# Hybrid encoder layer on one Trainium2 core: the short convolution's projections leave the head loop and become 2x2-block pairs, and GpSimd combines the two attention maps

## The reference

```python
proj = u @ w_in                      # u: normalised x; columns: h, b, c (512 each), q, k, v (512 each), gates (2048)
inner = cc * hc
conv = sum(pad(inner)[:, tap:tap + s] * conv_w[tap] for tap in range(3))
y_conv = (bc * conv) @ w_conv_out
# 4 heads, query blocks of 128 tokens, two maps per head
s1 = q1b @ k1.T * scale + bias;  s2 = q2b @ k2.T * scale + bias
a = softmax(s1) - lam * softmax(s2)
o = rmsnorm(a @ v) * (1 - lam_init)
y_attn = o @ w_attn_out
merged = g[0] * y_conv + g[1] * y_attn          # g = sigmoid(gates + b_gate)
x = x + norm(merged @ w_o)
x = x + norm(relu(norm(x) @ w_ff1) ** 2 @ w_ff2)
```

## Time and profile before

| | before |
|---|---|
| median of 3 runs | 1377.86 us (1377.61 to 1378.33) |
| span of the profiled execution | 1375.7 us |
| TensorE busy | 1366.8 us (99%) |
| VectorE busy | 980.2 us (71%) |
| ScalarE busy | 587.7 us |
| GpSimd busy | 109.6 us, 73 instructions |
| start of the gate pairs, of the branches | 458.06, 572.74 us |

### The profile page before, as it was taken

How to read it: one execution, slowest core, us unless ns; L and a number is a source line. 1 busy time by engine, 2 the same in 40 slices (tenths; PEclk the granted TensorE clock), 3 DMA queues, 4 the chain that set the end, 5 groups by cost and what they waited for, 6 DMA issues and landing times.

```text
span 1375.7 us, 17472 instructions
## 1 busy us (share of the span) xinstructions
PE 1366.8 (99%) x6377; PEld 1120.0 (81%) x6377; DVE 980.2 (71%) x1415; ACT 587.7 (43%) x907; POOL 109.6 (8%) x73
## 2 busy tenths in 40 slices
PE   9999999999999999999999999999999999999998
PEld 8778778778778888888888888888888888888886
DVE  7786786885999664667376886777664786765676
ACT  7443543543545454511243453333333444444453
POOL 0000000000000000000000333233333000000000
PEclk9999999999999999999999999999999999999999
DMA  5101111101111332455721354444445974345443
GB/s 188 47 27 31 36 31 30 46 15 46 30 29 62 100 125 99 142 151 171 254 79 60 107 179 150 161 149 150 153 146 210 362 269 111 96 124 191 114 130 108
DMA packets 141646, 162.04 MB, mean 118 GB/s; under 512 B 6861, under 2 KB 88970, under 8 KB 141450
## 3 DMA queue, kind: packets, MB, share of 16 engines
q1 hardware_dynamic: 135568, 148.27, 33.6%
q10 hardware_dynamic: 6010, 12.88, 2.4%
HBM read 114.98 MB, written 46.14 MB: 117 GB/s over the span
## 4 chain that ended last, share of the span: by engine, by line
PE 64%; DVE 1%; DMA 0%; ACT 0%; issue 0%; ACTq 0%; DVEq 0%
PE psum L1012 26%; PE psum L1166 22%; PE psum L886 13%; PE psum L1143 3%; PE psum L1115 1%; DVE v L2331 0%; DMA gates_scratch<-staging 0%; DVE y L2346 0%; ACT staging L1319 0%; DVE prod L1947 0%; DVE norms L2320 0%; ACTq L1322 0%; DVEq L291 0%; ACT w_hi L1345 0%; ACT prod L1368 0%
## 5 line engine op out<-in xcount | busy, mean ns | idle before, releaser
L1166 PE MATMUL psum<-op 128*128 128x512 f32 x1344 | 305.0, 389 | 0.1
L1166 PEld LDWEIGHTS psum<-op 128*128 128x128 f32 x1344 | 252.2, 188 | 52.8 <-issue 0.5
L886 PE MATMUL psum<-act_hi,w_hi 128*128 128x512 f32 x448 | 178.7, 399 | 1.1 <-DVE act_lo L1719 1.1
L886 PE MATMUL psum<-act_hi,w_lo 128*128 128x512 f32 x448 | 174.9, 390 | 0.0
L886 PE MATMUL psum<-act_lo,w_hi 128*128 128x512 f32 x448 | 174.4, 389 | 0.0
L2210 DVE TENSOR_TENSOR op<-v,op 128x512 fp32r<-128x512 f32 x112 | 78.6, 702 | 87.4 <-ACT op L1580 87.3
L1580 ACT ACTIVATE op<-v 128x512 fp32r<-128x512 f32 x112 | 70.7, 631 | 148.8 <-PE psum L1166 145.5
L886 PEld LDWEIGHTS psum<-act_hi,w_hi 128*128 128x128 f32 x448 | 84.2, 188 | 19.2 <-DVE w_lo L1725 1.7
L886 PEld LDWEIGHTS psum<-act_hi,w_lo 128*128 128x128 f32 x448 | 84.1, 188 | 18.2
L886 PEld LDWEIGHTS psum<-act_lo,w_hi 128*128 128x128 f32 x448 | 84.3, 188 | 16.3
L1819 DVE CUSTOM_DVE_ANT_0 e<-psum,alibi 128x1024 f32<-128x1024 f32 x64 | 78.1, 1221 | 11.1 <-issue 10.7
(11 more groups left out here) (271 smaller groups left out, 2787.6 us busy)
## 6 DMA issues: line engine op xcount, KB each, us to landing
f_raw<-f_scratch SPq DMA_DIRECT2D x112, 256.0 KB, 2.7
w_raw<-in_w_in SPq DMA_DIRECT2D x34, 512.0 KB, 4.6
w_raw<-in_w_ff SPq DMA_DIRECT2D x32, 512.0 KB, 4.9
f_scratch<-f_out SPq DMA_DIRECT2D x56, 256.0 KB, 2.3
v<-in_w_ff SPq DMA_DIRECT2D x12, 1024.0 KB, 7.9
gates_scratch<-staging ACTq DMA_DIRECT2D x32, 256.0 KB, 2.0
gate_in<-gates_scratch SPq DMA_DIRECT2D x16, 512.0 KB, 4.3
f_scratch<-staging SPq DMA_DIRECT2D x30, 256.0 KB, 2.2
```

The source lines that it names most:

```text
L886: mm = nc.tensor.matmul(bank, stat(a, kt), moving(b, kt), start=(n == 0), stop=(n == len(terms) - 1))
L1166: mm = nc.tensor.matmul(psum[:, (X_BANK, Z_BANK)[m % 2][t]], op[n % SLOTS][:, 2 + a, token_cols(t)], op[n % SLOTS][:, b], start=(m in (0, ...
```

## The change

The conv's panels h, c and b leave the head loop. For head i < 4 the panels h and c become pair i of the block scheme, the four b panels become pairs 4 and 5, and the six gate pairs follow as pairs 6 to 11 (`CONV_PAIRS = 6`). VectorE computes the conv from the pairs' results (`conv_step`).

The head loop keeps q, k and v. It is written as 8 steps in each head: scores of block n, one unit (`filler`), transpose of block n-1. The units of k and q in these steps are those of the next head, and the last head's free places take gate units 0 to 3. The sums of squares now stand in the middle of an AV unit. `at_lo` stands ahead of the maxima on VectorE.

The maps get two sets of buffers, `e[s][c]`, as do the small numbers. The weighted sum leaves VectorE: GpSimd scales each map (two tensor_scalar of 128x1024) and adds them (one tensor_tensor), for each of the 32 blocks. The token sums of the pairs (`t_sum`) are spread over the last head and the units behind it.

```diff
+def filler(i, n):
+    if i == 0 and n < 3:
+        return ((0, "q", 1), (0, "v", 0), (0, "v", 1))[n]
+    if n in LAST_FILL and i == HEADS - 1:
+        return (HEADS, "g", LAST_FILL[n])
+    return ((i, "v", 0), (i - 1, "AV", 1), (i, "v", 1), (i + 1, "k", 0), (i + 1, "k", 1), (i, "AV", 0), (i + 1, "q", 0),
+            (i + 1, "q", 1))[n]
...
-GATE = Pairs(GATE_PANELS // 2, KT - GATE_PANELS // 2, ("X2", "Z1", "X3", "Y", "X4", "Z2"), (0, 0))
+GATE = Pairs(0, CONV_PAIRS + KT - GATE_PANELS // 2, ("X2", "Z1", "X3", "Y", "X4", "Z2"), (0, 0))
...
+            for block in range(HEADS * QB):
+                s = block % 2
+                pool.wait_ge(combine, 2 * block + 2)
+                nc.gpsimd.tensor_scalar(e[s][1][:], e[s][1][:], weight2[s], None, ALU.mult).then_inc(a_ready, 1)
+                nc.gpsimd.tensor_scalar(e[s][0][:], e[s][0][:], recip[s][:, 0:1], None, ALU.mult).then_inc(a_ready, 1)
+                pool.wait_ge(a_ready, 3 * block + 2)
+                nc.gpsimd.tensor_tensor(e[s][0][:], e[s][0][:], e[s][1][:], ALU.add).then_inc(a_ready, 1)
...
-                        vec.tensor_scalar(e[1][:], e[1][:], weight2, None, ALU.mult).then_inc(combine, 1)
-                        dve.wait_ge(combine, blk * 3 + 3)
-                        vec.scalar_tensor_tensor(out=e[0][:], in0=e[0][:], scalar=recip[:, 0:1], in1=e[1][:],
-                                                 op0=ALU.mult, op1=ALU.add).then_inc(a_ready, 1)
...
+            for i in range(HEADS):
+                for n in range(QB):
+                    scores(i, n)
+                    unit(filler(i, n), (), (lambda: turn((i, "VT", 0))) if n == 3 else None)
+                    if n > 0:
+                        turn((i, "T", n - 1))
+                    elif i > 0:
+                        turn((i - 1, "T", 7))
...
+                    if n == 3:
+                        turned_lo((i, "VT", 0))
+                    if n == (0 if i else 1):
+                        panel_lo(HEAD_PANELS * (i + 1))
+                    elif n in (3, 5):
+                        panel_lo(HEAD_PANELS * (i + 1) + (n - 1) // 2)
+                    elif n == 2 and i > 0:
+                        av_copy(i - 1, 1)
+                    elif n == 6:
+                        av_copy(i, 0)
+                    weights(i, n)
+                    if i > 0:
+                        if n == 1:
+                            o_inverse(i - 1, 0)
+                        elif n == 2:
+                            o_squares_lo(i - 1, 1)
+                        elif n == 5:
+                            o_inverse(i - 1, 1)
+                    if n == 6:
+                        o_squares_lo(i, 0)
+                    if i == HEADS - 1 and n in (2, 4, 7):
+                        t_sum(GATE, 3, (2, 4, 7).index(n))
```

More of the change, by code:

```diff
@@ L83 @@
[L83 to L98, removed]
+PANELS = ["k", "q", "v"]
@@ L238, with panel_of, o_inside @@
 PASSES = ((0, 0), (0, 1), (1, 0))
[L241 to L265, removed]
+def panel_of(x):
+    i, kind, n = x
+    if kind == "g":
+        return HEADS * HEAD_PANELS + GATE_UNITS[n] // 2
+    return HEAD_PANELS * i + "kqv".index(kind)
+def o_inside(x):
+    i, kind, n = x
+    if kind != "AV" or (i, n) == (0, 0):
+        return None
+    return (i, 0) if n == 1 else (i - 1, 1)
+PANEL_READ = {}
+for _x in PROJ:
+    if _x[1] != "AV":
+        PANEL_READ[panel_of(_x)] = PROJ_AT[_x]
 WARM = (34, 6)
@@ L1008, in mix @@
+            last = HEADS - 1
+            unit((HEADS, "g", 4))
+            turn((last, "T", 7))
+            unit((HEADS, "g", 5))
+            unit((last, "AV", 1))
+            unit((HEADS, "g", 6))
+            pe.wait_ge(o_read, half_at(last, 0))
+            o_sum(psum[:, 1 - BANK_AT[last, "AV", 1] % 2], last, 1)
+            unit((HEADS, "g", 7))
             def mix(bank, stat, moving, first, last):
@@ new lines, in _ @@
+            for i in range(HEADS):
+                head(i)
+            last = HEADS - 1
+            copy_hi((HEADS, "g", 3))
+            turned_hi((last, "T", 6))
+            panel_hi(P_BR - 1)
+            t_hi_part(GATE, 3)
+            copy_hi((HEADS, "g", 4))
+            turned_hi((last, "T", 7))
+            copy_hi((HEADS, "g", 5))
+            o_deviation(last, 0)
+            o_squares(last, 1)
+            p = GATE.first
+            for x in ("W11", "W12"):
+                g_part_hi(x, p)
@@ new lines, in copy_lo, with maximum @@
+            def copy_lo(x):
+                i, kind, n = x
+                dve.wait_ge(qk_hi, QK_AT[x])
+                hi, lo = q_hl if kind == "q" else k_hl[i % 2]
+                vec.tensor_tensor(lo[:, half_cols[n]], unit_bank(x), hi[:, half_cols[n]].bitcast(F32), ALU.subtract
+                                  ).then_inc(qk_ready, 1)
+            def maximum(i, n, c):
+                block = block_at(i, n)
+                s = block % 2
+                if c == 1:
+                    if n == 0:
+                        dve.wait_ge(table_ready, i + 1)
+                    dve.wait_ge(s_done, block + 1)
+                    wait(dve, a_ready, 3 * (block - 1))
+                elif block > 1:
+                    dve.wait_ge(tb_done, TB_AT[(block - 2) // QB, "T", (block - 2) % QB])
+                vec.memset(spare, 0.0)
+                start = S - P - P * n
+                read = (s_read, map1_read)[c]
+                vec.tensor_tensor_reduce(
+                    out=e[s][c][:], in0=psum[:, SB + 2 * c:SB + 2 * c + 2].rearrange("p b c -> p (b c)"),
+                    in1=table[:, start:start + S], scale=1.0, scalar=-3.0e38, op0=ALU.add, op1=ALU.max,
+                    accum_out=maxima[s][:, c:c + 1]).then_inc(read, 1)
+                dve.wait_ge(read, block + 1)
+                vec.tensor_scalar(neg_max[s][:, c:c + 1], maxima[s][:, c:c + 1], -SCALE, None, ALU.mult
+                                  ).then_inc(max_ready, 1)
```

755 lines of the change are left out of this document (426 added, 329 removed).

## The result

The changed kernel takes 1414.46 us (1413.67 to 1415.68); the ratio to the kernel before is 1.0266 (interval 1.0251 to 1.0280), +36.6 us. The profiled execution has a span of 1413.1, +37.4.

The account below looks back on a forecast made before the run. TensorE, busy 1366.8 of 1375.7 us, was taken as the bound: 17.4 saved by fewer matmuls against waits of 40.0 gives +22.6, a span of 1398.3; medians lie 2.2 above, so 1400.5, with 1376 to 1424 for 8 in 10.

Parts of the forecast that it names:

- cover is taken away: Heads: removed units had covered VectorE and ScalarE catching up; TensorE now waits 40.0 us in sum, against -17.4.
- Start, 3.4: First scores: now after the third unit, TensorE is ready at about 33.7, VectorE's k low part at 37.1.
- Products with v, at least 1.07 each, seven times: AV0 in four heads, AV1 in three: waits for a transpose's low part, 7.5 us in all, called certain.
- the larger AV1 terms: Second product with v, three heads: waits 3.67, 2.98 and 2.98 in place of 1.07, the table instruction waiting for GpSimd.
- S7, 4.3: Scores of block 7, heads 1 to 3: 1.29 each, reciprocals and product delaying maxima; plus 0.46 at last head's block 4.
- one input on GpSimd, 1.3 us: GpSimd's scaling of a 128x1024 map: 1.3 us each, between 0.95 and 2.6, making a block 5.1.
- transposes that wait for GpSimd, 7.8: TensorE's transposes in the heads: waits of 1.8 in heads 1 and 2 each, 4.1 in head 3.
- the last block's 7.2: Last block's transpose: wanted at 14.2 after the last scores, GpSimd ends at 21.3 between token sums; 7.2 us.
- GpSimd becomes the bound: Rival, chance 0.08: one input costs like two, 2.6; a block is 7.8 of an 8.1 step; +54.4, 1432.
- the exclusion: GpSimd and VectorE's two-SBUF-input instructions, plus the table, wait for each other's whole instruction; the table case adds 2.9.
- The rival "faster": Chance 0.14: VectorE has slack in the heads, only certain waits of 10.9 stay; -6.5, 1371.4.
- No exclusion: Rival, chance 0.17: in the heads GpSimd runs beside VectorE at full pace, one input near 0.95; +5.3, 1383.2.

Follow-up runs that it names:

- experiment 1: Changed kernel without GpSimd's loop in the heads: maps neither weighted nor summed; 1383.98 us, ratio 1.0042 to the kernel before.
- 2: Changed kernel with GpSimd's two scalings left out, so it only adds the unweighted maps; 1393.96 us, ratio 1.0119 to the kernel before.
- 7: From experiment 1: an extra overwritten product of 24 matmuls ahead of seven products with v; 1407.68 us, ratio 1.0211 to the kernel before.
- experiment 3: Changed kernel with GpSimd's scalings and sum replaced by three memsets (0.95, 0.95, 0.42 us) that read nothing; 1384.95 us, ratio 1.0047.
- experiment 6: Changed kernel with VectorE scaling the second map; GpSimd scales the first and forms the sum; 1416.61 us, ratio 1.0280.
- `after`: The changed kernel itself, against the kernel before; 1414.46 us, ratio 1.0266.
- `const_scale`: Changed kernel with GpSimd's two scalings taking a constant in place of the weight in SBUF; 1413.91 us, ratio 1.0261.
- `bcast_mul`: Changed kernel with GpSimd's two scalings as tensor_tensor, the second input being the weight repeated along the row; 1414.86 us, ratio 1.0266.

## Why the prediction was right in its sign and its range, and low in its size

In steps, the shorter head without GpSimd costs 6.3 (experiment 1), the sum on GpSimd 10.0 more (2), the two scalings 20.5 more.

**Right: cover is taken away.** It was the larger statement of the prediction, and experiments 1 and 7 show it without GpSimd: +6.3 where 16.4 were saved, and 14.4 back with seven units. Term by term (the changed kernel's trace):
- *Start, 3.4*: 2.85, on `k_lo` as named.
- *Products with v, at least 1.07 each, seven times*: 0.88, 1.74, none, 0.88, none, 1.76, 0.86; 6.1 in all. Each of the two that are missing stands behind a transpose that had itself waited 2.09 and scores at the lower clock, which gave `at_lo` the time. The floor was right to 0.2 (0.86 to 0.88 for 1.07); the larger AV1 terms (9.6, measured 4.4) were too large, being built on a table instruction waiting 1.7 for GpSimd and a long row of VectorE behind it: the table took 1.55 and not 2.8.
- *S7, 4.3*: none. The product that was to wait 1.5 for GpSimd took 0.75 five times of six.

**Wrong in size: one input on GpSimd, 1.3 us.** That is the term that failed: 2.85 alone, 2.97 to 2.99 with what VectorE holds it up. A block is 8.1 to 8.4 and not 5.1. The upper bound itself, two inputs' 2.6, did not hold: I had argued that one input cannot cost more than two. It does here, 2.85 against 2.39 (1.89 with a repeated second input). So "transposes that wait for GpSimd, 7.8" became 20.7, and the last block's 7.2 became 5.6. The rival "GpSimd becomes the bound" (0.08) came nearest in the price of an instruction (2.6) and had too high a one of the whole (+54): GpSimd is not the bound, since in the heads it still waits 19 times for VectorE's weights, 39.7 us in all.

**Half right: the exclusion.** It is there, and experiments 2 and 3 show its price apart from GpSimd's length: the sum's reads cost 10 us, its length 1 at most. But it is not held for a tensor_scalar's whole length. In the changed kernel, VectorE's instructions that began while GpSimd ran (rows of GpSimd's and VectorE's timelines):

```profile
308.41 2.34 POOL L891 TENSOR_TENSOR e<-e,e 128x1024 f32<-128x1024 f32 x1
310.72 4.89 POOL L888 TENSOR_SCALAR e<-e,small 128x1024 f32<-128x1024 f32 x1
...
308.61 4.29 DVE L1976 TENSOR_TENSOR g_sum<-g_sum,act_lo 128x2048 f32<-128x2048 f32 x1
...
111.23 3.02 POOL L889 TENSOR_SCALAR e<-e,small 128x1024 f32<-128x1024 f32 x1
```

The token sum (2.29 alone) began 0.20 behind a tensor_tensor of 2.34 and took 4.29, 2.0 more: held to its end, near enough. The tensor_scalar behind it, begun at 310.72, took 4.89, 2.0 more: held till the token sum ended at 312.9. The table at 111.81 (its row stands in the section on the result) began 0.58 behind a tensor_scalar of 3.02 and took 1.55, 0.4 more: held till 0.98 into it and then free. The squares' low part, 0.67 behind the start of one, took 0.99 in place of 0.69, six times: till 0.97. The Trainium skill (SBUF — State Buffer, Who interferes with whom) has the pair held for the whole instruction. For the tensor_tensor the trace agrees (2.2 of 2.39); for the tensor_scalar it does not, 0.97 of 2.85. Its rule that fast one-input instructions of VectorE are held too, which no row of before showed, agrees: 1.52 for 0.75 in experiment 6. The hold goes both ways: the row at 310.72 is GpSimd held while VectorE's token sum runs.

**Missing: what a gap costs beyond its length.** The sum counted waits alone, 40.0; the trace has 38.2 over before (40.9 less 2.7), nearly the same, by other terms. What lifts +22.6 to +37.4 is the 15.7 us of busy time that came back, clock dips and restarts (and 1.0 more because I had taken 17.4 off and not 16.4, 1.9 less because the waits were fewer). I had named the clock as what would make the prediction too low, and given it no number. That the two totals of the waits agree is partly luck: the terms for GpSimd (15.0, measured 26.3) were 11 too small, those for AV and S7 (19.4, measured 6.1) 13 too large. The signs that I had named say the same: the head's period is 76.9, outside my 69 to 74, which was to mean that the table is wrong, and TensorE is busy 0.7 less and not 17.

**The rival "faster"** (-6.5) fails in experiment 1, which gives it the best case: even without GpSimd the kernel is 6.3 over. "No exclusion" (+5.3) is near what experiment 3 comes to, 7.0, but there GpSimd has no scalings and reads nothing.

No run here is faster than the kernel before. In experiment 1 the 16.4 us saved by pairs are worth less than the cover that the same units gave to a head. A version that keeps some units in the heads is the one to try; it wasn't built, and that it would gain is not shown.

## What to carry to other kernels

Where an engine is busy 99% of the time, the work on it is also the cover for all the others: before taking a piece away, count what lies beside it, and price every wait by its length and its restart. When work moves to GpSimd, count what its reads hold up on VectorE as well as its own length, and don't bound a one-input instruction there by a two-input one.

## What the runs showed of the hardware

- GpSimd's tensor_scalar of 128x1024 float32 took 2.85 us undisturbed with the scalar in SBUF and 2.77 with a constant (`after`, `const_scale`); tensor_tensor 2.39; tensor_tensor with the second input repeated from one column 1.89 (`bcast_mul`); memset 0.95.
- GpSimd's tensor_scalar kept VectorE's two-input and fast one-input instructions out for its first 0.9 to 1.0 us only, a tensor_tensor for about 2.2 of its 2.39. Memsets did not hold two-input ones (0.69 and 2.28, as alone); the one-input table, begun 0.04 behind a memset of 0.42, took 1.39 in place of 1.15, twice (`memset_hold`).
- After five gaps of TensorE of 1.8 to 5.6 us the granted clock was at the lower level for about 3.4 us (6.9 at the gap of 5.6), but not after each such gap: 2.09 at 81.69, 1.78 at 261.94 and 2.21 at 310.80 had none.
